# Rotary swap of queries and keys: from TensorE products with a permutation matrix to DMAs between partitions

## The chip, the cores and the metric

One core of one Trainium2 chip runs the whole program. The metric is the time of one execution on the device in microseconds, the median of several runs. Short names of the engines as the profile has them: PE (TensorE), DVE (VectorE), ACT (ScalarE), POOL (GpSimd), SP (SyncE, here only a queue of DMAs).

## What is computed

Two blocks one after the other on a sequence of 512 tokens of width 2048, in float32. The first, an mLSTM and a spatial gating unit with their projections, is not touched. The second has two hybrid layers over 528 tokens (16 meta tokens ahead): a long convolution, sliding window attention and a recurrent unit, side by side. The part around the change, cut to what matters:

```
def _partial_rotary(x, pos):                      # heads of 64, ROT_DIM = 16, half = 8
    ang = pos[:, None] * inv_freq[None, :]
    x1 = x[..., :half]
    x2 = x[..., half:ROT_DIM]
    rot = concatenate([x1 * cos - x2 * sin, x2 * cos + x1 * sin])
    return concatenate([rot, x[..., ROT_DIM:]])

q = _partial_rotary(q.reshape(B, L, N_HEADS, HEAD_DIM), pos)     # 16 heads
k = _partial_rotary(k.reshape(B, L, N_KV, HEAD_DIM), pos)        # 4 heads
att = _sliding_window_sink_attention(q, k, v, attn_sinks)
```

Only the first 16 features of each head are rotated: feature d is mixed with feature d + 8.

## The kernel before, in words

Features lie on partitions, tokens in the free dimension. A tile of 128 partitions holds two heads of 64, so the rotation mixes partitions 0 to 7 with 8 to 15 and 64 to 71 with 72 to 79.

Every projection is a run of *units*. A unit makes 256 output features in two passes of 128 (m = 0, 1), each over four *pieces* of the weights (j = 0 to 3, four tiles of 128 input features each). A product of two float32 numbers is made of three float32r products (`three`, L493 to L498), of a high and a low part of weights and inputs. SP loads the raw pieces (`load`), ACT rounds piece j to `w_high` (`high`, L884), DVE subtracts to get `w_low` (`low`, L1311), PE waits for that (`arrive`, L517) and multiplies. `high(U, j)` needs piece j of the unit before to be used up in both passes. With `wide=True` a pass has 96 products of 264 columns. ACT takes the sums out of PSUM (`take`, L898).

A layer first makes the keys (unit O_K) and values (O_V), then four groups of four heads each. Group g has the units V (queries), V+1 (convolution inputs), V+2 (attention gate), V+3 (recurrent inputs); V of the next group is the last unit, V+4, in the code of a group. The order of everything else is written out by hand on each engine. On PE small work is hung behind the pieces of these units by `hook` (`behind`, L806): at n = 8, behind piece 0 of unit V+1, `rotate(0)` and `rotate(1)`; at n = 11, behind piece 3 and so at the end of the first pass, the first `score` (L720); further scores, transposes (`turn`) and value products follow, one behind each piece; behind unit V+4 come the last of them and the products of the recurrent gates (`recur`).

The rotary step before: `rotate` (L707) multiplies both query tiles of a group, `qrw[:, t]`, by the permutation `rot`, whose entries are 1 and -1, into PSUM banks 4 to 7, four float32 products of 264 columns. DVE's `rope` (L1702) then multiplies that by `sin`, the tile by `cos`, and adds. `rotate_k` (L687) and the loop at L1636 do the same for the two tiles of keys, once in a layer.

On ACT a group begins at L1177: it takes query tile 0 out (L1178), copies values and keys for the products (`values`, `keys`), makes `w_high` of unit V+1 in between, takes query tile 1 out (L1185) and makes piece 3. Before that stand, from the group before, the two gates of the recurrent unit, tanh, exp and square root (L1232 to L1240). DVE's part of a group begins with the four `w_low` of unit V+1, then both ropes (L1712 to L1714). PE's loop over groups has three turns and one group behind it; ACT's has two turns of two groups. Both DMA queues are in use: SP's for weights, ACT's for the residual stream, constants and parameters of a layer.

`y2` (y_layer) holds the outputs of the layer, 16 tiles: Y_ATT 0 to 7, Y_LRU 8 to 11, Y_CONV 12 to 15.

Of the kernel before, what the change touches and what calls it, by code (L numbers as in the profile page):

```python
# [22 lines left out]
ALU = mybir.AluOpType  # L23
AX = mybir.AxisListType
ds = bass.ds

P = 128
# [17 lines left out]
LH = L // 2  # L45
# [4 lines left out]
HD = 64  # L50
NKV = 4
GROUP = 4
NH = NKV * GROUP
BLK = 128
# [23 lines left out]

K_IDENT, K_ONES, K_TRI, K_ROT = 0, P, 2 * P, 3 * P
K_MASK0 = 4 * P  # L80
K_MASK = K_MASK0 + NM + BLK
# [20 lines left out]
def program(nc, a, out):  # L102
# [14 lines left out]
    with ExitStack() as ctx:  # L117
# [102 lines left out]
        shape_at = rr.at  # L220
        kshape = rr.take("shape_constants", [P, K_ALL - K_ROT])
        rot = kshape[:, 0:P]
        ma0 = kshape[:, K_MASK0 - K_ROT:K_MASK - K_ROT]
        mas = kshape[:, K_MASK - K_ROT:K_CAUS - K_ROT]
        mca = kshape[:, K_CAUS - K_ROT:K_COS - K_ROT]
        cos = kshape[:, K_COS - K_ROT:K_SIN - K_ROT]
        sin = kshape[:, K_SIN - K_ROT:K_ALL - K_ROT]
        mo = rr.take("meta_out", [P, NM])
# [37 lines left out]
        def sem(name):  # L266
# [41 lines left out]
            sem("shape_in"), sem("pl_in"), sem("pl_tr"), sem("pl_ok"), sem("sink_in"))  # L308
        rot_mm, rope_done, rotk_mm, k_roped = sem("rot_mm"), sem("rope_done"), sem("rotk_mm"), sem("k_roped")
        kz_ready, vz_ready, mo_ready = sem("kz_ready"), sem("vz_ready"), sem("mo_ready")  # L310
# [181 lines left out]
        def _(pe):  # L492
# [185 lines left out]
            with pe.Fori(0, LAYERS) as l:  # L678
# [7 lines left out]

                def rotate_k():  # L687

                    pe.wait_ge(evac, 2 * (U + O_K) + 2)
                    pe.wait_ge(shape_in, 16 * (l + 1))  # L690
                    pe.wait_ge(pl_ok, l + 1)
                    for t in range(2):
                        for q in range(2):
                            last = pe.matmul(ps[:, 4 + 2 * t + q, 0:LH], rot, krw[:, t, q * LH:(q + 1) * LH], start=True, stop=True)
                        last.then_inc(rotk_mm, 1)

                unit_tokens(U + O_V, fill, 0, [
                    [(ps[:, i // 2, i % 2 * 256:(i % 2 + 1) * 256], NM + i * P) for i in range(ST)],
                    [(ps[:, 2, 0:256], 0)]], after=(rotate_k, None))
                unit(U + O_GRP, fill, wide=True)  # L700

                def group(g, ending=None):
# [3 lines left out]

                    def rotate(t):  # L707

                        if t == 0:
                            pe.wait_ge(evac, 2 * V + 2)  # L710
                            pe.wait_ge(k_roped, 2 * (l + 1))

                            pe.wait_ge(r_act, 2 * G)
                            pe.wait_ge(o_taken, 2 * G)
                            pe.wait_ge(mo_ready, 2 * G)
                        for q in range(2):
                            last = pe.matmul(ps[:, 4 + 2 * t + q, 0:LH], rot, qrw[:, t, q * LH:(q + 1) * LH], start=True, stop=True)
                        last.then_inc(rot_mm, 1)

                    def score(i, n):  # L720
                        q = qrw[:, i // 2, :]
                        bank = 4 + n % 2
                        if n == 0 and i == 0:
                            pe.wait_ge(rope_done, 2 * G + 2)
                            pe.wait_ge(kz_ready, G + 1)

                        pe.wait_ge(s_taken, 4 * A + 4 * i + n + 1)
                        tq = NM + n * BLK
                        w = NM + (2 if n else 1) * BLK
                        last = pe.matmul(ps[:, bank, 0:w], q[:, tq:tq + BLK], kz[:, i % 2, max(n - 1, 0), 0:w],  # L730
                                         start=True, stop=True)
                        if n == 0:
                            last = pe.matmul(ps[:, bank, 160:160 + NM], q[:, 0:BLK], kz[:, i % 2, 0, 0:NM],
                                             start=True, stop=True)
                        last.then_inc(s_done, 1)

                    def turn(i, n):
                        if n == 0:
                            pe.wait_ge(p_ready, A + i + 1)

# [65 lines left out]
                    def behind(first):  # L806

                        def hook(n):
                            n += first
                            if n == 8:  # L810
                                rotate(0)
                                rotate(1)
                            elif n >= 11:
                                step(n - 11)
                        return hook
# [67 lines left out]
        def _(act):  # L883
# [187 lines left out]
            with act.Fori(0, LAYERS) as l:  # L1071
# [6 lines left out]

                act.dma_start(kshape[:], consts[:, K_ROT:K_ALL]).then_inc(shape_in, 16)
                row = 0  # L1080
# [30 lines left out]
                act.wait_ge(res_out, 16 * (l + 1))  # L1111
                act.wait_ge(k_roped, 2 * (l + 1))

                def group(gp, s):
# [62 lines left out]
                    act.wait_ge(s_done, 4 * A)  # L1177
                    take(V, 0, two(qrw[:, 0, :]), halves(0))  # L1178
                    values()
                    high(V + 1, 0)  # L1180
                    keys(0)
                    high(V + 1, 1)
                    keys(1).then_inc(kz_ready, 1)
                    high(V + 1, 2)
                    take(V, 1, two(qrw[:, 1, :]), halves(2))  # L1185
                    high(V + 1, 3)
                    act.wait_ge(c_taken, G)
# [121 lines left out]
        def _(dve):  # L1309
# [299 lines left out]
            with dve.Fori(0, LAYERS) as l:  # L1609
# [26 lines left out]
                for m in range(2):  # L1636
                    k = krw[:, m, :]
                    dve.drain()
                    dve.wait_ge(rotk_mm, 2 * l + m + 1)
                    dve.tensor_tensor(two(t1[:]), halves(4 + 2 * m), two(sin), ALU.mult)  # L1640
                    dve.tensor_tensor(k, k, cos, ALU.mult)
                    dve.drain()
                    dve.tensor_tensor(k, k, t1[:], ALU.add).then_inc(k_roped, 1)  # L1643

                with dve.Fori(0, NKV) as g:
# [56 lines left out]
                    def rope(t):  # L1702

                        q = qrw[:, t, :]
                        dve.drain()
                        dve.wait_ge(rot_mm, 2 * G + t + 1)
                        dve.tensor_tensor(two(t1[:]), halves(4 + 2 * t), two(sin), ALU.mult)
                        dve.tensor_tensor(q, q, cos, ALU.mult)
                        dve.drain()
                        dve.tensor_tensor(q, q, t1[:], ALU.add).then_inc(rope_done, 1)  # L1710
# [140 lines left out]
def shape_constants():  # L1851
# [7 lines left out]
    half = HD // 4 // 2  # L1859
    for o in (0, HD):  # L1860
        for d in range(half):
            c[o + half + d, K_ROT + o + d] = -1.0
            c[o + d, K_ROT + o + half + d] = 1.0
    neg = np.float32(-1e30)
# [9 lines left out]
    for o in (0, HD):  # L1874
        for q in (0, half):
            c[o + q:o + q + half, K_COS:K_SIN] = np.cos(ang).T
            c[o + q:o + q + half, K_SIN:K_ALL] = np.sin(ang).T
    return c
# [22 lines left out]
```

## Time and profile before

| | |
|---|---|
| median of 3 runs | 3525.28 us (3524.44 to 3526.98) |
| the profiled execution, its own time | 3524.65 us |
| its span, first to last instruction | 3522.6 us |
| mean granted TensorE clock | 0.978 |
| busy: PE, DVE, ACT, POOL | 95%, 48%, 37%, 9% |
| the three products of `three`, each | 5280 instructions |
| DMA queue of ACT | 2592 packets, 19.18 MB, 1.4% |
| DMA queue of SP | 338944 packets, 281.09 MB, 26.2% |

How to read it: PE records overlap, since one product is fed in while the one before drains, so busy times of lines on PE add up to more than the span; the distance from start to start tells the cost. The two layers stand in the span at about 1800 to 2650 us and 2650 to 3480 us, their groups of heads at about 1900 to 2400 and 2740 to 3240 us.

### The profile page before, as it was taken

What the parts mean: (1) busy time and instruction counts of PE and PEld (TensorE: products, weight loads), DVE (VectorE), ACT (ScalarE), POOL (GpSimd) and SP (SyncE); (2) the same over time, 40 slices, a digit from 0 to 9 for tenths busy, and PEclk for the clock granted to TensorE, in tenths of its full rate; (3) what the DMA queues carried; (4) which work ended last, traced back from release to release, by engine and by line L of the source; (5) the groups of instructions that cost most, each with busy time, mean ns of one, the idle gap of its engine ahead of it and who ended that gap; (6) DMA issues with size and microseconds to landing.
All of it is one profiled execution on the core that took longest, in us unless ns stands there. A gap on an engine that the chain in (4) does not pass through costs nothing.

```text
span 3522.6 us, 58033 instructions
## 1 busy us (share of the span) xinstructions
PE 3354.9 (95%) x21518; PEld 3031.3 (86%) x21518; DVE 1702.0 (48%) x2289; ACT 1310.0 (37%) x2069; POOL 315.4 (9%) x320
## 2 busy tenths in 40 slices
PE   6999999999999999899969999999996999999996
PEld 5888988888888888788849999999996999999995
DVE  5332233334443434325683555556545455555555
ACT  3332233233333333323242554545224445545422
POOL 2000000000000000000000331330000214312000
PEclk9999999999999999999979999999997999999997
DMA  5332233233232323322213222223323222221421
GB/s 183 96 90 89 83 95 95 84 95 99 80 101 77 101 77 92 124 95 95 95 54 127 73 74 74 68 72 113 99 72 108 85 74 62 73 73 61 145 95 48
DMA packets 346082, 316.88 MB, mean 90 GB/s; under 512 B 18785, under 2 KB 339321, under 8 KB 344001
## 3 DMA queue, kind: packets, MB, share of 16 engines
q1 hardware_dynamic: 338944, 281.09, 26.2%
q10 hardware_dynamic: 2592, 19.18, 1.4%
q0 software_dynamic: 4400, 14.62, 1.2%
q8 instruction: 98, 1.61, 0.2%
q14 instruction: 48, 0.39, 0.0%
HBM read 297.74 MB, written 17.07 MB: 89 GB/s over the span
## 4 chain that ended last, share of the span: by engine, by line
PE 39%; issue 13%; DVE 3%; ACT 1%; DMA 1%; POOLq 1%; POOL 1%; DVEq 0%; ACTq 0%
PE ps L496 11%; PE ps L497 11%; PE ps L498 11%; PE ps L771 1%; PE ps L730 1%; DMA residual_stream<-y_layer 1%; DVE residual L1576 1%; DVE residual L1587 0%; PE ps L745 0%; PE ps L778 0%; PE ps L802 0%; PE ps L668 0%; PE ps L749 0%; DVE w_low L1314 0%; ACT x_high L1017 0%
## 5 line engine op out<-in xcount | busy, mean ns | idle before, releaser
L496 PE MATMUL ps<-x_high,w_high 128*128 128x264 f32 (+1 forms) x5280 | 1738.3, 329 | 65.9 <-DVE x_low L1595 47.5
L497 PE MATMUL ps<-x_low,w_high 128*128 128x264 f32 (+1 forms) x5280 | 1707.8, 323 | 0.0
L498 PE MATMUL ps<-x_high,w_low 128*128 128x264 f32 (+1 forms) x5280 | 1703.6, 323 | 0.0
L1314 DVE TENSOR_TENSOR w_low<-w_raw,w_high 128x1024 fp32r<-128x1024 f32 x524 | 640.7, 1230 | 1152.1 <-ACT w_high L890 1126.6
L496 PEld LDWEIGHTS ps<-x_high,w_high 128*128 128x128 f32 x5280 | 1000.5, 189 | 155.7 <-DVE x_low L1595 45.9
L497 PEld LDWEIGHTS ps<-x_low,w_high 128*128 128x128 f32 x5280 | 1000.7, 190 | 84.1 <-issue 3.8
L498 PEld LDWEIGHTS ps<-x_high,w_low 128*128 128x128 f32 x5280 | 997.3, 189 | 77.7
L890 ACT ACTIVATE w_high<-w_raw 128x1024 fp32r<-128x1024 f32 x524 | 551.7, 1058 | 730.6 <-PE ps L498 612.4
L502 PE MATMUL ps<-w_high,x_high 128*128 128x256 f32 x1184 | 333.1, 281 | 2.0 <-ACT w_spatial_rowsum L937 2.0
L503 PE MATMUL ps<-w_high,x_low 128*128 128x256 f32 x1184 | 333.1, 281 | 0.0
L504 PE MATMUL ps<-w_low,x_high 128*128 128x256 f32 x1184 | 333.0, 281 | 0.0
L502 PEld LDWEIGHTS ps<-w_high,x_high 128*128 128x128 f32 x1184 | 222.7, 188 | 3.7 <-issue 2.8
L504 PEld LDWEIGHTS ps<-w_low,x_high 128*128 128x128 f32 x1184 | 223.3, 189 | 0.0
L503 PEld LDWEIGHTS ps<-w_high,x_low 128*128 128x128 f32 x1184 | 222.6, 188 | 0.8
L1689 DVE SCALAR_TENSOR_TENSOR c_partial<-c_raw,par,c_partial 128x528 f32<-128x528 f32 x168 | 141.0, 839 | 30.3 <-issue 30.3
L901 ACT ACT_TABLE_LOAD x86 | 110.3, 1283 | 23.7 <-DVE k_roped L1643 11.8
L1657 DVE SCALAR_TENSOR_TENSOR p_block<-ps,shape_constants 128x272 f32<-128x272 f32 (+1 forms) x128 | 51.9, 406 | 136.5 <-PE ps L730 90.6
L427 POOL DMA_DIRECT2D gate_bc<-gate_rows x8 | 4.3, 532 | 1205.6 <-DVE y_m L1469 666.8
L473 POOL TENSOR_TENSOR y_layer<-y_layer,tmp 128x528 f32 x64 | 104.4, 1631 | 9.9 <-issue 9.9
L901 ACT ACTIVATE out_tmp_layer<-ps 128x528 f32<-128x528 f32 x32 | 19.3, 602 | 176.8 <-PE ps L498 176.8
L480 POOL TENSOR_TENSOR c_raw<-c_raw,a_gate_silu 128x528 f32<-128x528 f32 x8 | 8.9, 1118 | 791.1 <-ACT a_gate_silu L901 791.1
L471 POOL TENSOR_TENSOR tmp<-c_raw,par 128x528 f32<-128x528 f32 x64 | 78.1, 1220 | 14.5 <-issue 14.5
(331 smaller groups left out, 2623.9 us busy)
## 6 DMA issues: line engine op xcount, KB each, us to landing
w_raw<-in_w_in SPq DMA_DIRECT2D x776, 256.0 KB, 3.0
w_raw<-in_w_out SPq DMA_DIRECT2D x256, 256.0 KB, 2.9
residual_stream<-y_layer ACTq DMA_DIRECT2D x2, 4224.0 KB, 13.2
residual<-residual_stream ACTq DMA_DIRECT2D x8, 1056.0 KB, 11.5
x_natural<-in_x SPq DMA_DIRECT2D x4, 1024.0 KB, 8.8
x_feature_major<-x_stage POOLq DMA_DIRECT2D x16, 256.0 KB, 4.0
gate_bc<-gate_rows POOLq DMA_DIRECT2D x8, 512.0 KB, 4.5
acc<-x_feature_major POOLq DMA_DIRECT2D x1, 4096.0 KB, 13.3
```

What stands on the lines that cost most here:

```text
L471: pool.tensor_tensor(t1[:], cra[:, j:j + L], wj, ALU.mult)
L473: ins = pool.tensor_tensor(ct, ct, t1[:], ALU.add)
L496: pe.matmul(dst, wh[:, j, kt, wc], xh[:, k, tok], start=first, stop=False)
L497: pe.matmul(dst, wh[:, j, kt, wc], xl[:, k, tok], start=False, stop=False)
L498: return pe.matmul(dst, wl[:, j, kt, wc], xh[:, k, tok], start=False, stop=last)
L502: pe.matmul(dst, xh[:, k, tok], wh[:, j, kt, :], start=first, stop=False)
L503: pe.matmul(dst, xl[:, k, tok], wh[:, j, kt, :], start=False, stop=False)
L504: return pe.matmul(dst, xh[:, k, tok], wl[:, j, kt, :], start=False, stop=last)
L890: act.activation(wh[:, j], raw[:, j], ACT.Copy).then_inc(hi_ready, 1)
L901: act.activation(dst, src, fn, **kw).then_inc(evac, 1)
L1314: dve.tensor_tensor(wl[:, j], raw[:, j], f(wh[:, j]), ALU.subtract).then_inc(lo_ready, 1)
L1689: dve.scalar_tensor_tensor(cacc[:], cra[:, j:j + L], wj, cacc[:], ALU.mult, ALU.add)
```

## The change

The swap of partitions is made by DMAs from SBUF to SBUF, issued by ACT. For a tile, `swap` issues four: 8 rows of 528 floats each, from rows 8 to 15 to rows 0 to 7 and back, for both heads of the tile. They go into rows of `y2` that are free at that time: Y_ATT + 2g + t for query tile t of group g (semaphore `q_swapped[t]`, 64 for a tile), Y_LRU + m for key tile m (`k_swapped`, 128 for both). ACT drains after each `take` of queries and then issues the four. The signs of the permutation move into the constants (`-sin` in the upper rows of each head), rows of the tile that aren't swapped meet a sine of zero. DVE reads the swapped tile from `y2` rather than from PSUM. PE loses `rotate` and `rotate_k`; the waits in them go or move to `score` and `turn`. ACT's wait for `k_roped` moves from ahead of the groups to ahead of `keys(0)`. The constants loaded in a layer are 128 columns fewer.

```diff
@@ tensor
-                def rotate_k():
-                    pe.wait_ge(evac, 2 * (U + O_K) + 2)
-                    pe.wait_ge(shape_in, 16 * (l + 1))
-                    pe.wait_ge(pl_ok, l + 1)
-                    for t in range(2):
-                        for q in range(2):
-                            last = pe.matmul(ps[:, 4 + 2 * t + q, 0:LH], rot, krw[:, t, q * LH:(q + 1) * LH], start=True, stop=True)
-                        last.then_inc(rotk_mm, 1)
...
-                    def rotate(t):
-                        if t == 0:
-                            pe.wait_ge(evac, 2 * V + 2)
-                            pe.wait_ge(k_roped, 2 * (l + 1))
-                            pe.wait_ge(r_act, 2 * G)
-                            pe.wait_ge(o_taken, 2 * G)
-                            pe.wait_ge(mo_ready, 2 * G)
-                        for q in range(2):
-                            last = pe.matmul(ps[:, 4 + 2 * t + q, 0:LH], rot, qrw[:, t, q * LH:(q + 1) * LH], start=True, stop=True)
-                        last.then_inc(rot_mm, 1)
...
                             pe.wait_ge(rope_done, 2 * G + 2)
                             pe.wait_ge(kz_ready, G + 1)
+                            pe.wait_ge(pl_ok, l + 1)
+                            pe.wait_ge(r_act, 2 * G)
...
                         if n == 0:
+                            pe.wait_ge(mo_ready, 2 * G)
                             pe.wait_ge(p_ready, A + i + 1)
...
-                            if n == 8:
-                                rotate(0)
-                                rotate(1)
-                            elif n >= 11:
+                            if n >= 11:
                                 step(n - 11)
@@ scalar
-                act.wait_ge(k_roped, 2 * (l + 1))
+                def swap(dst, src, done):
+                    for o in (0, HD):
+                        for a0, a1 in ((0, RD), (RD, 0)):
+                            act.dma_start(dst[o + a0:o + a0 + RD, :], src[o + a1:o + a1 + RD, :]).then_inc(done, 16)
+                for m in range(2):
+                    swap(y2[:, Y_LRU + m, :], krw[:, m, :], k_swapped)
...
                     take(V, 0, two(qrw[:, 0, :]), halves(0))
+                    act.drain()
+                    swap(y2[:, ds(Y_ATT + 2 * g, 1), :].squeeze(1), qrw[:, 0, :], q_swapped[0])
                     values()
                     high(V + 1, 0)
+                    act.wait_ge(k_roped, 2 * (l + 1))
                     keys(0)
                     high(V + 1, 1)
                     keys(1).then_inc(kz_ready, 1)
                     high(V + 1, 2)
                     take(V, 1, two(qrw[:, 1, :]), halves(2))
+                    act.drain()
+                    swap(y2[:, ds(Y_ATT + 2 * g + 1, 1), :].squeeze(1), qrw[:, 1, :], q_swapped[1])
                     high(V + 1, 3)
@@ vector, the same for the keys with k_swapped, 128 * (l + 1)
                         q = qrw[:, t, :]
                         dve.drain()
-                        dve.wait_ge(rot_mm, 2 * G + t + 1)
-                        dve.tensor_tensor(two(t1[:]), halves(4 + 2 * t), two(sin), ALU.mult)
+                        dve.wait_ge(q_swapped[t], 64 * (G + 1))
+                        dve.tensor_tensor(t1[:], y2[:, ds(Y_ATT + 2 * g + t, 1), :].squeeze(1), sin, ALU.mult)
@@ constants
-            c[o + q:o + q + half, K_SIN:K_ALL] = np.sin(ang).T
+            c[o + q:o + q + half, K_SIN:K_ALL] = np.sin(ang).T if q else -np.sin(ang).T
```

## Rows read from the trace of the kernel before

**Rows 1.** Page, part 1: busy us (share of the span) and instructions by engine
```profile
PE 3354.9 (95%) x21518; PEld 3031.3 (86%) x21518; DVE 1702.0 (48%) x2289; ACT 1310.0 (37%) x2069; POOL 315.4 (9%) x320
```

**Rows 2.** Timeline (start us, duration us, instruction), PE around the keys' rotation
```profile
1888.37 0.28 PE L504 MATMUL ps<-w_low,x_high 128*128 128x256 f32 x1
...
1890.38 0.28 PE L503 MATMUL ps<-w_high,x_low 128*128 128x256 f32 x1
```

**Rows 3.** Timeline of ACT, group 1 to 2 of layer one
```profile
2165.13 0.59 ACT L901 ACTIVATE q_roped<-ps 128x528 f32<-128x528 f32 x1
2165.62 1.05 ACT L890 ACTIVATE w_high<-w_raw 128x1024 fp32r<-128x1024 f32 x1
```

**Rows 4.** Timeline of DVE there: w_low pieces 0 and 3, ropes' first and last
```profile
2160.61 1.23 DVE L1314 TENSOR_TENSOR w_low<-w_raw,w_high 128x1024 fp32r<-128x1024 f32 x1 [3.20 <-ACT w_high L890]
...
2166.70 1.23 DVE L1314 TENSOR_TENSOR w_low<-w_raw,w_high 128x1024 fp32r<-128x1024 f32 x1 [0.22 <-ACT w_high L890]
2168.19 0.71 DVE L1707 TENSOR_TENSOR tmp<-ps,shape_constants 128x528 f32<-128x528 f32 x1 [0.26 <-PE ps L717]
...
2171.86 0.71 DVE L1710 TENSOR_TENSOR q_roped<-q_roped,tmp 128x528 f32<-128x528 f32 x1
```

**Rows 5.** Timeline of PE there: first product of V+1, first score
```profile
2161.90 0.39 PE L496 MATMUL ps<-x_high,w_high 128*128 128x264 f32 x1 [2.95 <-DVE w_low L1314]
...
2176.66 0.41 PE L730 MATMUL ps<-k_zero_padded,q_roped 128*128 128x144 f32 x2
```

**Rows 6.** Waits of PE, 1880 to 3200 us: total us, times, longest
```profile
PE ps L717 <- ACT q_roped L901: 2.4, 3, 1.0
```

**Rows 7.** Timeline of ACT's queue: DMA issues at the start of layer one
```profile
1856.19 1.09 ACTq L1087 DMA_DIRECT2D par_rows_layer<-in_lru_conv_b  x1
...
1860.38 0.26 ACTq L1087 DMA_DIRECT2D par_rows_layer<-in_lru_lambda  x1
1860.81 0.36 ACTq L1089 DMA_DIRECT2D small<-in_attn_sinks  x1
```

**Rows 8.** Timeline of ACT: an activation behind a drain
```profile
2027.69 0.74 ACT L1236 ACTIVATE r_tanh<-r_gate_a,small 128x528 f32<-128x528 f32 x1 [0.17 <-issue]
```

**Rows 9.** Windows (stretch, length, busy by engine, PEclk, DMA), group 1 to 2, layer two
```profile
2997.60:3015.40 17.80, 15.18 (x107) 14.73 (x106) 8.96 (x10) 7.49 (x20) 0.00 (x0) 0.90 0.40 120
```

**Rows 10.** Timeline of DVE, layer one: last rope and w_low piece 0, other groups
```profile
1926.81 0.71 DVE L1710 TENSOR_TENSOR q_roped<-q_roped,tmp 128x528 f32<-128x528 f32 x1
...
2036.57 1.23 DVE L1314 TENSOR_TENSOR w_low<-w_raw,w_high 128x1024 fp32r<-128x1024 f32 x1
...
2047.61 0.71 DVE L1710 TENSOR_TENSOR q_roped<-q_roped,tmp 128x528 f32<-128x528 f32 x1
...
2280.66 1.22 DVE L1314 TENSOR_TENSOR w_low<-w_raw,w_high 128x1024 fp32r<-128x1024 f32 x1
...
2291.63 0.71 DVE L1710 TENSOR_TENSOR q_roped<-q_roped,tmp 128x528 f32<-128x528 f32 x1
```

**Rows 11.** Timeline of PE, layer one: starts of V+1 and first scores, other groups
```profile
1932.53 0.41 PE L730 MATMUL ps<-k_zero_padded,q_roped 128*128 128x144 f32 x2
...
2039.85 0.36 PE L496 MATMUL ps<-x_high,w_high 128*128 128x264 f32 x1 [1.68 <-DVE w_low L1314]
...
2053.33 0.41 PE L730 MATMUL ps<-k_zero_padded,q_roped 128*128 128x144 f32 x2
...
2296.40 0.41 PE L730 MATMUL ps<-k_zero_padded,q_roped 128*128 128x144 f32 x2
```

**Rows 12.** Timeline of ACT, layer one: last copy of values, first copy of keys
```profile
1897.17 0.36 ACT L901 ACTIVATE v_tokens<-ps 128x256 f32<-128x256 f32 x1
...
1911.62 1.01 ACT L1125 ACTIVATE k_zero_padded<-k_roped 64x256 f32 x3
```

**Rows 13.** DMA issues by line: count, KB each, median us from issue to landing
```profile
residual<-residual_stream ACTq DMA_DIRECT2D x8, 1056.0 KB, 11.5
...
w_x_diag<-in_lru_wx POOLq DMA_DIRECT2D x16, 16.0 KB, 1.9
```

More of the change, by code:

```diff
@@ L52 @@
 GROUP = 4
+RD = HD // 8
 NH = NKV * GROUP
@@ L76 @@
 Y_ATT, Y_LRU, Y_CONV = 0, 8, 12
-K_IDENT, K_ONES, K_TRI, K_ROT = 0, P, 2 * P, 3 * P
-K_MASK0 = 4 * P
+K_IDENT, K_ONES, K_TRI = 0, P, 2 * P
+K_MASK0 = 3 * P
 K_MASK = K_MASK0 + NM + BLK
@@ L220, in program @@
         shape_at = rr.at
[L221 to L227, printed above, removed]
+        kshape = rr.take("shape_constants", [P, K_ALL - K_MASK0])
+        ma0 = kshape[:, K_MASK0 - K_MASK0:K_MASK - K_MASK0]
+        mas = kshape[:, K_MASK - K_MASK0:K_CAUS - K_MASK0]
+        mca = kshape[:, K_CAUS - K_MASK0:K_COS - K_MASK0]
+        cos = kshape[:, K_COS - K_MASK0:K_SIN - K_MASK0]
+        sin = kshape[:, K_SIN - K_MASK0:K_ALL - K_MASK0]
         mo = rr.take("meta_out", [P, NM])
@@ L308, in program @@
             sem("shape_in"), sem("pl_in"), sem("pl_tr"), sem("pl_ok"), sem("sink_in"))
-        rot_mm, rope_done, rotk_mm, k_roped = sem("rot_mm"), sem("rope_done"), sem("rotk_mm"), sem("k_roped")
+        q_swapped, rope_done, k_swapped, k_roped = [sem(f"q_swapped{t}") for t in range(2)], sem("rope_done"), sem("k_swapped"), sem("k_roped")
         kz_ready, vz_ready, mo_ready = sem("kz_ready"), sem("vz_ready"), sem("mo_ready")
@@ L685, in _ @@
                 pe.transpose(ps[:, 5, 0:ROWS_L2], prow2[0:ROWS_L2, 1, :], ident[0:ROWS_L2, 0:ROWS_L2]).then_inc(pl_tr, 1)
-                def rotate_k():
-                    pe.wait_ge(evac, 2 * (U + O_K) + 2)
-                    pe.wait_ge(shape_in, 16 * (l + 1))
-                    pe.wait_ge(pl_ok, l + 1)
-                    for t in range(2):
-                        for q in range(2):
-                            last = pe.matmul(ps[:, 4 + 2 * t + q, 0:LH], rot, krw[:, t, q * LH:(q + 1) * LH], start=True, stop=True)
-                        last.then_inc(rotk_mm, 1)
                 unit_tokens(U + O_V, fill, 0, [
                     [(ps[:, i // 2, i % 2 * 256:(i % 2 + 1) * 256], NM + i * P) for i in range(ST)],
-                    [(ps[:, 2, 0:256], 0)]], after=(rotate_k, None))
+                    [(ps[:, 2, 0:256], 0)]])
                 unit(U + O_GRP, fill, wide=True)
@@ L1077, in _ @@
                 act.dma_start(x_res, y2[:]).then_inc(res_out, 16)
-                act.dma_start(kshape[:], consts[:, K_ROT:K_ALL]).then_inc(shape_in, 16)
+                act.dma_start(kshape[:], consts[:, K_MASK0:K_ALL]).then_inc(shape_in, 16)
                 row = 0
@@ L1638, in _ @@
                     dve.drain()
-                    dve.wait_ge(rotk_mm, 2 * l + m + 1)
-                    dve.tensor_tensor(two(t1[:]), halves(4 + 2 * m), two(sin), ALU.mult)
+                    dve.wait_ge(k_swapped, 128 * (l + 1))
+                    dve.tensor_tensor(t1[:], y2[:, Y_LRU + m, :], sin, ALU.mult)
                     dve.tensor_tensor(k, k, cos, ALU.mult)
@@ L1859, in shape_constants @@
     half = HD // 4 // 2
[L1860 to L1863, printed above, removed]
+    assert half == RD
     neg = np.float32(-1e30)
```

## The prediction

> **What bounds the kernel now.** I read the page first: PE is busy for 95% of the span [rows 1], so a change counts only where PE works less or stands longer. The edit touches one stage, the attention groups of the two layers (from about 1850 to 2300 us and again from 2690 to 3140 us), so the rest was read there: PE's timeline around the products that go, PE's waits, then ACT's, DVE's and PE's timelines of the same places side by side. The reader is to see two things. First, the price of a rotation on PE: the last ordinary product before the rotation of the keys starts at 1888.37 and the pitch is 0.12; the second ordinary one after it starts at 1890.38, where it would have started at 1888.61 [rows 2]. So 1.77 us for four fp32 products and the change over to them and back. The rotation of a group's queries shows the same. Second, who is late where the groups change. In the first group of a layer ACT waits for PE between its pieces. In the other three ACT has just finished the gates of the group before, and takes the queries out, copies keys and makes w_high one behind the other without a pause: the second q_roped at 2165.13, w_high piece 3 at 2165.62, before the copy has ended [rows 3]. DVE's first w_low starts at 2160.61 and ends 1.23 later, at 2161.84 [rows 4], and PE, idle for 2.95 us, starts at 2161.90 [rows 5]: PE hangs on ACT there. PE then also waited for q_roped before three of the eight rotations, 2.4 us in all [rows 6].
>
> **What goes.** On PE one rotation of keys and four of queries in each layer: ten times 1.77, at most 17.7 us, and the 2.4 us of waits. The waits that stood in `rotate` move to `score` and `turn`; each but `rope_done` is for something finished long before. DVE's three products per half stay as they are; the operand read from PSUM is read from SBUF, and 0.71 us for the form with the PSUM operand (L1707) stands beside 0.71 for the one with both in SBUF (L1710) [rows 4], so I take no difference.
>
> **What comes.** All of it on ACT's queue. After each of the two q_roped copies of a group: a drain, then four DMA issues, then the work that was next. ACT's own queue shows what an issue costs: a transfer of 4 rows took 0.26 us, one of 128 rows 0.36, with 0.1 to 0.2 of register work between them; behind large transfers in flight the form of 4 rows took 1.09 [rows 7]. Nothing large is in flight on that queue in the groups, and a swap has 8 rows, so I take 0.27 and 0.1 for registers: 0.37 from one issue to the next. A drain shows as 0.17 of idle time between two activations [rows 8]. So d, by which the next operation of ACT comes later: the copy must end (0.59), drain 0.17, four issues 1.48, restart 0.1, together 2.34; before, the next one started 0.49 after the copy's start [rows 3]. d = 1.9 us. Its bounds: issues every 0.28, d = 1.4; every 1.09, d = 4.7. The drain matters, because without it issues could run under a copy.
>
> **Where d is on the path.** Two clocks run from a group change to its first score (L730): PE's, from its first product of unit V+1 through 96 products, and the ropes', ACT's copies, w_low piece 3, then two ropes on DVE. The score starts at the later one. The first d shifts everything that ACT does; the second shifts w_high piece 3 and so w_low piece 3, and the ropes stand behind that on DVE. So the ropes end 2d = 3.8 later, less some 0.1 that DVE no longer waits for PE's rotation (its wait of 0.26 before 2168.19 against 0.17 for a drain) [rows 4].
>
> Group 1 to 2 (called change 2): w_low piece 0 ends at 2161.84 + 1.9 = 2163.7; PE's way from there to the score was 14.76, of it 1.77 rotation and 1.0 the wait before it, leaving 12.0 [rows 5, 6]: 2175.7. Ropes: 2171.86 + 0.71 + 3.7 = 2176.3 [rows 4]. PE's idle time before V+1 grows from 3 to 5 us, and in layer two the same place, with a shorter pause, was followed by products at half pace: mean granted clock 0.90 over that 17.8 us [rows 9], that is 3.4 us at 1.2 instead of 2.4 GHz and 1.5 to 1.7 us lost. I count that loss in both layers now: PE 2177.2, against 2176.66 before, +0.5. In layer two it was already there; the first d and the rotation cancel: 0. Together +0.5.
>
> Change 1 (group 0 to 1): ropes 2047.61 + 0.71 + 3.7 = 2052.0, PE 2053.33 - 1.77 = 2051.6 [rows 10, 11]. PE's start of V+1 does not move, because it started at 2039.85, while w_low piece 0 had ended at 2036.57 + 1.23 = 2037.8, 2.0 us ahead: PE's loop jumps back there. Saved 2053.33 - 2052.05 = 1.3, twice: -2.5. Change 3: ropes 2291.63 + 0.71 + 3.7 = 2296.05, PE 2280.66 + 1.23 + 1.9 + 12.0 = 2295.8, against 2296.40 [rows 10, 11]: -0.3, twice: -0.6.
>
> First group: ACT has pauses, so only the second d counts: ropes end by 1926.81 + 0.71 + 1.9 = 1929.4, while PE comes at 1932.53 - 1.77 = 1930.8 [rows 10, 11]. All 1.77 is gained, twice: -3.5. If that cover of 1.4 us is gone, each us more costs one.
>
> Keys: eight issues after v_tokens (ends 1897.5), so until 1900.6; landed by 1903; both ropes 4.4 (as the queries' from 2168.19 to 2172.57 [rows 4]): 1907.4. First needed by the key copies at 1911.62 [rows 12]. Cover 4 us; -1.77 twice: -3.5.
>
> The landing of a swap: 16 KB by the nearest small transfers took 1.9 us, 1056 KB took 11.5 [rows 13]; a swap is four of 16.5 KB, so 2 to 3 us from the last issue. The second swap's last issue is at about 2165.72 + 1.9 + 1.65 = 2169.3, and the second rope wants it at 2168.19 + 2.27 + 3.7 = 2174.2: 4.9 us of cover, which is why I count the transfer itself at nothing.
> By the Trainium skill ("DMA: Bandwidth & Descriptors", section "Anatomy of one DMA", measured for GpSimd's path) a DMA has a fixed cost of about 2.0 us, most of it the write receipt, and its bandwidth section wants transfers batched, those under 64 KB being dominated by descriptors; that speaks against moving 16 rows in four pieces, and the trace's 1.9 us agrees with the fixed part. Overlapped, it would change nothing here; one behind the other it is the third rival below.
>
> **Sum** against the profiled run's own 3524.65 us (span 3522.6): -3.5 (keys) -3.5 (first group) -2.5 +0.5 -0.6 = -9.6, so 3515.0. The median of the runs is 0.6 above the profiled one: 3515.6. Of the 20.1 us that PE gets back, half is handed to ACT.
>
> **Rivals.**
> 1. Forecast, issues at 0.33 to 0.45 us: 3510 to 3521, taken 3515.6. Chance 0.46.
> 2. Dearer issues, slower than before: ACT's queue at the three late changes. With d = 4.7 the ropes end 9.3 later: change 1 +4.3, change 2 +5.2, change 3 +5.2, first group -0.3, keys -1.8: +12.6 a layer, 3550. The three late changes give 12 us for each us of d; the sum is zero at d = 2.8, an issue of 0.61, and 7 us slower at 0.75. For it: nine of twelve such transfers cost about 1 us (one is shown) [rows 7]; against: those stood behind 5 MB. Chance 0.13.
> 3. The four transfers don't overlap: 4 x 1.9 = 7.6 us after the drain, the second rope starts 1.2 later than DVE could, six times: +7; keys 8 x 1.9 hold ACT's key copies by 6 us and the first score by 1.5: +3. Together 3525, no change. Against: issues come every 0.37 us and other queues have many in flight. Chance 0.09. This is what the batching rule would make of it.
> 4. Clock: after 5 us of idle time PE stays at half speed twice as long at change 2, or drops at change 3 too (idle 1.7 there): 1.5 to 1.7 us for each of two to four places beyond the cover of the ropes (0.7): 3518.5 to 3521, no change. Chance 0.13.
> 5. Cheaper, d = 1.4: change 1 gives the full 1.77, change 3 1.3, change 2 0.8: 3508. Chance 0.19.
>
> **Numbers.** A measurement of this kernel tells about 0.2% (7 us) from no change; faster means below 3518.2. Faster: nine tenths of 1 and all of 5 less a little, 0.58. Same: the rest of 1, 3 and 4, 0.28. Slower: 2 and some of 3, 0.14. Range 3507 to 3530: from the cheap case to an issue of about 0.7 us; only the worse part of 2 and what is better than 5 is left out.
>
> **What would show it.** Right: no L694 or L717; PE's idle time before V+1 about 5 us at change 2 and about 1.7 at change 3; DMA issues of about 0.3 us on ACT's queue with a hole of some 2.3 us after each q_roped; a short wait of PE L730 for DVE's ropes in three of four groups; DVE never long waiting for a swap. Wrong: ropes that wait for DMA (3), issues of over 0.6 (2), no wait before L730 and PE's idle time as before (5), more than 7 us of granted clock 0.5 in the groups of a layer (4). The sum falls as a whole if ACT can issue under its copies, or if its pause at the jump back of its own loop (change 2) grows with the longer code.

## The result, and the profile after

The changed kernel takes 3537.1 us (median of 7 runs, 3536.5 to 3539.7); the kernel before took 3525.3 in the runs between them (7 runs, 3524.3 to 3529.3). The ratio is 1.0033, 95% interval 1.0021 to 1.0044: 0.33% slower, where 0.27% faster was forecast, and outside of the range of 3507 to 3530. The profiled run has a span of 3535.5 us against 3522.6.

The page of the kernel after, its span and part 1 (answers [rows 1]):

```profile
span 3535.5 us, 57971 instructions
PE 3348.4 (95%) x21438; PEld 3024.7 (86%) x21438; DVE 1703.0 (48%) x2289; ACT 1310.7 (37%) x2069; POOL 315.4 (9%) x320
```

The rotations are gone, ten with four float32 products each; the trace shows a float32 product as two records, so eighty are missing, and PE is busy for 6.5 us less. Nothing else on that page names the loss: ACT is not busier, because a DMA issue is not counted as busy. One has to look at the places where the groups change. The same change from group 1 to 2 as in [rows 3], timeline of ACT in the kernel after (start us, us, instruction, idle time before and its releaser):

```profile
2159.08 0.61 ACT L878 ACTIVATE q_roped<-ps 128x528 f32<-128x528 f32 x1
2159.85 3.05 ACTq L1094 DMA_DIRECT2D y_layer<-q_roped  x4
2163.04 0.42 ACT L1119 ACTIVATE v_zero_padded<-v_tokens 128x256 f32 x1 [3.35 <-issue]
...
2169.49 0.59 ACT L878 ACTIVATE q_roped<-ps 128x528 f32<-128x528 f32 x1
2170.24 3.03 ACTq L1094 DMA_DIRECT2D y_layer<-q_roped  x4
2173.38 1.06 ACT L867 ACTIVATE w_high<-w_raw 128x1024 fp32r<-128x1024 f32 x1 [3.30 <-issue]
```

Four issues hold ACT's queue for 3.05 us; 77 of the 80 in the trace last 0.67 to 0.72 us (the others 0.76, 0.80 and 1.16), and with the register instruction between them they start every 0.775 us. The forecast had 0.37. The operation behind the first copy starts 3.96 us after it, where it started 0.49 after it before [rows 3]: d is 3.47 here for the first half and 3.89 - 0.49 = 3.40 for the second, against 1.9 in the forecast. In what follows d is taken as 3.44, the mean of the two.

DVE there (answers [rows 4]), from w_low piece 0 to the end of the ropes:

```profile
2164.98 1.23 DVE L1304 TENSOR_TENSOR w_low<-w_raw,w_high 128x1024 fp32r<-128x1024 f32 x1 [6.55 <-ACT w_high L867]
...
2174.47 1.23 DVE L1304 TENSOR_TENSOR w_low<-w_raw,w_high 128x1024 fp32r<-128x1024 f32 x1 [3.63 <-ACT w_high L867]
2176.09 0.71 DVE L1697 TENSOR_TENSOR tmp<-y_layer,shape_constants 128x528 f32<-128x528 f32 x1 [0.39 <-issue]
...
2179.82 0.71 DVE L1700 TENSOR_TENSOR q_roped<-q_roped,tmp 128x528 f32<-128x528 f32 x1
```

And PE there (answers [rows 5]), and PE's waits of the whole run:

```profile
2166.26 0.59 PE L496 MATMUL ps<-x_high,w_high 128*128 128x264 f32 x1 [6.30 <-DVE w_low L1304]
...
2180.93 0.51 PE L709 MATMUL ps<-k_zero_padded,q_roped 128*128 128x144 f32 x2 [1.41 <-DVE q_roped L1700]
```

```profile
PE ps L496 <- DVE w_low L1304: 22.9, 6, 6.3
...
PE ps L709 <- DVE q_roped L1700: 9.6, 6, 2.0
```

The reader is to see the hole of ACT twice. The first opens PE's wait for w_low (6.3 us here; all such waits of the run were 8.8 us and are 22.9 now), the second makes w_low piece 3 late, and the ropes behind it, so that PE waits at the first score too, in all six late groups. DVE itself does not wait for a swap: the 0.39 us before the first rope is "issue", no DMA. At the keys the wait is for DMA, and it is covered (timelines of ACT and DVE, kernel after):

```profile
1897.55 5.69 ACTq L1094 DMA_DIRECT2D y_layer<-k_roped  x8
```

```profile
1904.73 0.71 DVE L1630 TENSOR_TENSOR tmp<-y_layer,shape_constants 128x528 f32<-128x528 f32 x1 [6.40 <-DMA y_layer<-k_roped]
```

Where the 12.9 us of span came from, by the time of each group's first score in the two traces (after less before, and the step from one score to the next):

| place | layer one | layer two | forecast, each |
|---|---|---|---|
| keys and first group | -3.4 | -3.5 | -3.5 |
| change 1 | +2.7 | +2.9 | -1.25 |
| change 2 | +3.35 | +3.4 | +0.5, 0 |
| change 3 | +3.7 | +3.7 | -0.3 |

That is +12.8. Beside it stand +1.6 before 1850 us, in work that both kernels share, +1.6 in layer one's last group, where the granted clock is 0.5 for 3.4 us, and -1.4 between the layers and -1.8 behind the second one; they sum to nothing.

### The profile page after: what moved, and what is told of

The parts are those of the page before. It is cut to its first block, busy times and chain, and to the rows that moved or that the text cites. A ratio compares the mean times of both kernels' runs of the same rounds, so it can differ in the third digit from the quotient of the medians.

```text
span 3535.5 us, 57971 instructions
## 1 busy us (share of the span) xinstructions
PE 3348.4 (95%) x21438; PEld 3024.7 (86%) x21438; DVE 1703.0 (48%) x2289; ACT 1310.7 (37%) x2069; POOL 315.4 (9%) x320
## 4 chain that ended last, share of the span: by engine, by line
PE 39%; issue 14%; DVE 3%; ACT 1%; DMA 1%; POOLq 1%; POOL 1%; DVEq 0%; ACTq 0%
PE ps L496 11%; PE ps L497 11%; PE ps L498 11%; PE ps L751 1%; PE ps L709 1%; DMA residual_stream<-y_layer 1%; DVE residual L1566 1%; DVE residual L1577 0%; PE ps L725 0%; PE ps L758 0%; PE ps L782 0%; PE ps L668 0%; PE ps L729 0%; DVE w_low L1304 0%; ACT x_high L994 0%
## 5 line engine op out<-in xcount | busy, mean ns | idle before, releaser
L709 PE MATMUL ps<-k_zero_padded,q_roped 128*128 128x272 f32 (+1 forms) x256 | 73.4, 368 | 9.6 <-DVE q_roped L1700 9.6
## 6 DMA issues: line engine op xcount, KB each, us to landing
residual_stream<-y_layer ACTq DMA_DIRECT2D x2, 4224.0 KB, 13.2
residual<-residual_stream ACTq DMA_DIRECT2D x8, 1056.0 KB, 11.7
```

## The experiments

Theory: ACT's queue is held by the issues, at a price of 0.775 us for each, and all of the loss is in the two holes of each group. Rivals: the transfers or their landing; the drains; what was taken away from PE (its clock, the waits that were moved). Medians of before in the sessions below are 3526.3 to 3527.3; ratios are against the runs of the same session.

**Take the swaps away.** In the changed kernel:

```diff
-                    act.drain()
-                    swap(y2[:, ds(Y_ATT + 2 * g, 1), :].squeeze(1), qrw[:, 0, :], q_swapped[0])
...
-                        dve.wait_ge(q_swapped[t], 64 * (G + 1))
+                        dve.wait_ge(evac, 2 * V + t + 1)
```

> The changed kernel without its DMA swaps and without the two drains before them; DVE waits only for the copy q_roped (or k_roped) itself and reads whatever stands in y_layer, so the swap is left out of the computation. It shows what taking the rotation off PE is worth by itself. Theory (the whole loss is the time that ACT spends issuing): ten rotations of 1.77 us and up to 2.4 us of waits come back, nothing else moves: 18 to 20 us faster than the kernel before, 3505 to 3507 us. Rival (PE gets nothing from the missing products, because the ropes or the clock take it): within 8 us of before, 3517 or more.

Measured: 3506.2 us, ratio 0.9941 (0.9924 to 0.9957). As the theory has it: the rotation on PE was worth 21 us, and the additions take more than that back.

**Add the swaps alone**, to the kernel before:

```diff
+                    act.drain()
+                    swap(y2[:, ds(Y_ATT + 2 * g, 1), :].squeeze(1), qrw[:, 0, :], q_swapped[0])
...
                         dve.wait_ge(rot_mm, 2 * G + t + 1)
+                        dve.wait_ge(q_swapped[t], 64 * (G + 1))
```

> The kernel before, its PE rotation kept and still used, with the drains and all DMA swaps added on ACT's queue; DVE waits for both. It shows the cost of the additions alone. Theory: the next operation of ACT comes 3.4 us later twice in each group; the late changes give, in each layer, about +1.8 (change 1), +5.0 (change 2, of it 1.6 for clock), +3 (change 3), and 0 to +1.5 in the first group, the keys hidden: 20 to 23 us slower, 3545 to 3548 us. Rival (the loss comes from what was taken away, for instance waits moved to the score, or from PE's emptier queue and its clock): within 5 us of before.

Measured: 3545.9 us, ratio 1.0055 (1.0038 to 1.0072). With PE's rotation in place the additions cost 19 us, and PE's waits for w_low are the 22.9 us of the changed kernel, though nothing was taken from PE. What was removed or moved on PE is no cause: taking it away is a gain with the swaps (3545.9 to 3537.1) as without them. But the two effects don't add up; -21 and +19 would make -2, where the change measures +12. With the rotation PE comes to the first score late enough never to wait there; without it 17.7 us of products go and the 9.6 us of waits at the score come.

**Half of the issues:**

```diff
-                    for o in (0, HD):
+                    for o in (0,):
```

> The changed kernel with two of the four DMAs of each swap (the second head's rows are not swapped, which leaves half of the swap out). Theory (each issue holds ACT 0.775 us, so d falls from 3.44 to 1.9 us, and each us of d is worth 12 us): 3516 us, 3512 to 3520. Rival (a fixed part of the swap, its drain, the wait for the landing or the restart of ACT, carries the loss): less than half of the difference between the changed kernel and no_swaps goes, 3522 to 3535 us.

Measured: 3518.6 us, ratio 0.9977 (0.9967 to 0.9986), inside the theory's range. Timeline of ACT in this kernel, from group 0 to 1:

```profile
2030.63 0.59 ACT L878 ACTIVATE q_roped<-ps 128x528 f32<-128x528 f32 x1
2031.38 1.49 ACTq L1094 DMA_DIRECT2D y_layer<-q_roped  x2
2033.02 0.42 ACT L1119 ACTIVATE v_zero_padded<-v_tokens 128x256 f32 x1 [1.79 <-issue]
```

d is 2.39 - 0.49 = 1.9 here, the value that the forecast took for four issues, and the gain over the kernel before is 8.1 us by the ratio, where the forecast had 9.7. The hole is 0.30 us longer than its issues, with two of them (1.79 and 1.49) as with four (3.35 and 3.05): that is all that is left for the drain and the restart, so the drain is not the loss; no run takes it out alone. Three points give the slope, each taken against the kernel before of its own session: -20.8 us at d = 0, -8.1 at 1.9, +11.6 at 3.44. The first 1.9 us cost 6.7 us each and the next 1.54 cost 12.8 each. So the "12 us for each us of d" was right where all three late changes hang on it, and the point of no change lies at 1.9 + 8.1/12.8 = 2.5, where the forecast had 2.8.

**The same transfers from another queue.** SP issues them, behind its loads of unit V+1; ACT neither drains nor issues. The keys' swaps go to SP as well, behind the loads of the values, and go out at 1866 rather than at 1897.55, so they too are hidden:

```diff
+                    for m in range(2):
+                        sp.wait_ge(evac, 2 * V + m + 1)
+                        swap(y2[:, ds(Y_ATT + 2 * g + m, 1), :].squeeze(1), qrw[:, m, :], q_swapped[m])
```

> The changed kernel with the same sixteen-row swaps issued from SP's queue instead of ACT's; ACT neither drains nor issues, SP waits for each copy. Theory (ACT's issue time, not the transfers): ACT's copies, w_high and w_low run as in the kernel before, the swap of the second half lands some 4.5 us after its copy ends, about when DVE's second rope could start, so nearly all of the gain stays: 3505 to 3511 us. Rival (the transfers themselves, their landing or the traffic of 8-row pieces cost the time): 3525 to 3537 us, as in the changed kernel. A second rival: SP's weight loads, now behind the swaps in its queue, come late, and PE waits for them: 3515 us or more, with PE's new waits on weights.

Measured: 3503.3 us, ratio 0.9934 (0.9917 to 0.9950), some 2 us under the theory's range, below the kernel before by 24 us in the medians and, by the two ratios, below the changed one by 35, with the whole computation in it. It is even a little under the kernel without swaps, whose clock fell at change 2 in both layers, where here it did not; at change 1 it fell here in both layers, there in one. PE's waits for w_low, timelines of SP and of DVE at change 2, kernel with swaps on SP:

```profile
PE ps L509 <- DVE w_low L1304: 9.5, 4, 2.7
```

```profile
2154.79 9.91 SPq L355 DMA_DIRECT2D y_layer<-q_roped  x8
2165.05 1.21 SPq L349 DMA_DIRECT2D w_raw<-in_w_in  x2
```

```profile
2162.54 1.23 DVE L1304 TENSOR_TENSOR w_low<-w_raw,w_high 128x1024 fp32r<-128x1024 f32 x1 [0.22 <-ACT w_high L880]
2164.15 0.71 DVE L1697 TENSOR_TENSOR tmp<-y_layer,shape_constants 128x528 f32<-128x528 f32 x1 [0.39 <-issue]
...
2166.48 0.71 DVE L1697 TENSOR_TENSOR tmp<-y_layer,shape_constants 128x528 f32<-128x528 f32 x1 [0.22 <-issue]
```

The issues are no cheaper on SP (0.65 to 0.74 us each); they hold a queue that has time. The second swap's last issue ends at about 2164.7, and the second rope starts at 2166.48 without a wait. The price is that the loads of unit V+2 now go out at 2165.05, over 7 us after w_low piece 0 ended (2157.69), where they were issued 0.2 us after it before; PE doesn't wait for weights anywhere in these groups. So the transfers, their landing and their traffic cost nothing, and the rival of transfers one behind the other falls with them.

**Which hole does what.** The swap of one half on ACT as in the change, that of the other half and the keys' on SP:

```diff
                     take(V, 0, two(qrw[:, 0, :]), halves(0))
+                    act.drain()
+                    swap(y2[:, ds(Y_ATT + 2 * g, 1), :].squeeze(1), qrw[:, 0, :], q_swapped[0])
```

> The changed kernel with the first half's swap (and its drain) on ACT's queue as in the change, and the keys' and the second half's from SP's queue. Theory (two clocks): one d of 3.44 us ahead of w_high piece 0 shifts both PE's start of the next unit and the ropes. Against the kernel with all swaps on SP: change 1 +0.2, change 2 +3.4 to 5, change 3 +2.7 in each layer: 3516 to 3520 us. If only the sum of the issues counted, wherever they stand, both halves would give the same, about 3514.

> The changed kernel with the second half's swap (and its drain) on ACT's queue, and the keys' and the first half's from SP's queue. Theory (two clocks): this d stands behind PE's start, and only w_high piece 3, w_low piece 3 and the ropes come 3.44 us later. Against all swaps on SP: change 1 +0.2, change 2 +2.0, change 3 +1.1 in each layer: 3508 to 3512 us. If only the sum of the issues counted: about 3514, as with the first half.

Measured: first half on ACT 3525.0 us, ratio 0.9993 (0.9984 to 1.0003); second half 3517.1, ratio 0.9971 (0.9961 to 0.9982). Both miss their numbers by 5 us or more; equal they are not. PE at change 2 of layer one, first with the first half's swap on ACT:

```profile
2162.10 0.59 PE L509 MATMUL ps<-x_high,w_high 128*128 128x264 f32 x1 [6.45 <-DVE w_low L1312]
...
2176.05 0.41 PE L722 MATMUL ps<-k_zero_padded,q_roped 128*128 128x144 f32 x2
```

then with the second half's on ACT:

```profile
2159.55 0.39 PE L509 MATMUL ps<-x_high,w_high 128*128 128x264 f32 x1 [2.70 <-DVE w_low L1312]
...
2174.41 0.51 PE L722 MATMUL ps<-k_zero_padded,q_roped 128*128 128x144 f32 x2 [2.08 <-DVE q_roped L1708]
```

These are the two clocks of the prediction, one at a time. The first hole stands ahead of PE's start (6.45 us of waiting, none at the score), the second behind it (2.70 as before, and 2.08 at the score). The ratios put the first half at 21 us over the kernel with all swaps on SP and the second at 13, together 34 of the 35 that both cost. The sizes that were expected were off for these reasons. After the long pause the first kernel needs 13.95 us from 2162.10 to the score, where the kernel with all swaps on SP needs 11.71. Windows of the two (stretch, length, busy by engine, PEclk, DMA):

```profile
2162.10:2176.00 13.90, 13.90 (x96) 13.90 (x97) 7.75 (x9) 4.72 (x10) 0.00 (x0) 0.82 0.38 112
```

```profile
2154.00:2169.40 15.40, 12.74 (x105) 12.53 (x105) 8.97 (x10) 8.41 (x22) 0.00 (x0) 1.00 0.23 64
```

So the clock took 2.2 us there and, by the same two times, 2.5 in layer two, against the 0 to 1.6 that I had allowed; and 1.5 us of the first kernel's time lie behind the last score of layer two, where its granted clock is 0.5 for 3.4 us and that of the kernel with swaps on SP is not. In the second kernel the ropes cost more than worked out. They had less room than I took: in the kernel with swaps on SP they end 0.87 us ahead of the score at change 2 and 1.19 at change 3, where +2.0 and +1.1 from a d of 3.44 need 1.4 and 2.3. From their end to a score that waits for them are 0.35 to 0.5 us, which I had at nothing, and change 3 of layer one has a stretch of half clock (1.6 us) ahead of it.

**Issues under a running activation.** The four issues moved behind the next w_high, the drain replaced by a wait for the copy:

```diff
-                    act.drain()
-                    swap(y2[:, ds(Y_ATT + 2 * g, 1), :].squeeze(1), qrw[:, 0, :], q_swapped[0])
                     values()
                     high(V + 1, 0)
+                    act.wait_ge(evac, 2 * V + 1)
+                    swap(y2[:, ds(Y_ATT + 2 * g, 1), :].squeeze(1), qrw[:, 0, :], q_swapped[0])
```

> The changed kernel with each query swap's four issues moved behind the next w_high piece (piece 0 for the first half, piece 3 for the second), and in place of the drain a wait for the copy's own semaphore. If ACT's sequencer issues DMAs while an activation runs, some 1 us of the 3.1 of issues lies under w_high and the drain's tail is gone: d falls from 3.44 to about 2.1 for each half and piece 3 of w_high is no longer behind the second swap at all, so the ropes come some 4 us earlier: 3512 to 3520 us. If an issue cannot overlap a running activation, d stays over 3 and only the second half's moves behind piece 3: 3522 to 3530 us.

Measured: 3511.8 us, ratio 0.9956 (0.9939 to 0.9973), at the lower end of the first range. ACT at change 2:

```profile
2156.24 0.61 ACT L878 ACTIVATE q_roped<-ps 128x528 f32<-128x528 f32 x1
2156.75 0.41 ACT L1119 ACTIVATE v_zero_padded<-v_tokens 128x256 f32 x1
2156.98 0.72 ACTq L1094 DMA_DIRECT2D y_layer<-q_roped  x1
...
2157.58 1.06 ACT L867 ACTIVATE w_high<-w_raw 128x1024 fp32r<-128x1024 f32 x1
2157.82 2.23 ACTq L1094 DMA_DIRECT2D y_layer<-q_roped  x3
2160.27 1.03 ACT L1110 ACTIVATE k_zero_padded<-k_roped 64x256 f32 x3 [1.63 <-issue]
```

The first issue starts while the small copies run and the next under w_high: the queue goes on past an activation that has been handed over. The hole shrinks to 1.63 us, and w_high piece 0 is no longer behind it. Without leaving ACT, 27 of the changed kernel's 32 us over the kernel without swaps are back (by the ratios), and the issues are as many and each as dear. Place and drain were changed together here; what each gives was not measured. What is still missing against the swaps on SP is in part the landing, which is no longer hidden: DVE waits for the second half's swap before its second rope in all eight groups (10.2 us in all, up to 1.9 us; 0.95 at change 2), and PE waits 4.1 us at the score.

**What makes an issue dear.** Thirteen more DMAs of other forms behind the keys' eight swaps, one line each:

```diff
+                act.dma_start(y2[0:8, Y_LRU + 2, :], krw[8:16, 0, :]).then_inc(k_swapped, 16)
+                act.dma_start(y2[16:20, Y_LRU + 2, :], krw[8:12, 0, :]).then_inc(k_swapped, 16)
...
+                act.dma_start(y2[:, Y_CONV + 3, :], x_res[:, 0, :]).then_inc(k_swapped, 16)
```

> The changed kernel with thirteen more DMAs on ACT's queue behind the eight of the keys, each of another form and all into parts of y_layer or DRAM that nobody reads; DVE waits for them too. They are, in order, between buffers on the chip: 8 rows of 528 numbers, 4 rows, 1 row, 16 rows, 128 rows of 528, 8 rows of 512, 8 rows of 128, 4 rows of 128, 128 rows of 128; then 4 rows of 128 and 8 rows of 528 from DRAM, 8 rows of 528 to DRAM, 128 rows of 528 from DRAM. It prices one issue by its form. Theory 1 (the price is in what is described, rows and their length): few rows are cheap, 16 rows of 528 dearer than 8, 128 rows dearest. Theory 2 (the price is in the source, on the chip or in DRAM): all from the chip cost 0.65 to 0.7 us and those from DRAM 0.27 to 0.37. Theory 3 (few rows are cut into pieces for the 16 DMA engines, and that costs): the forms with fewer than 16 rows cost 0.65, those of 16 and 128 rows 0.27 to 0.37. The time of the whole is about 10 us a layer above the changed kernel at most, and is not what is asked.

> The kernel with the thirteen further forms again, now in the opposite order and ahead of the keys' eight swaps: first 128 rows of 528 from DRAM, 8 rows of 528 to DRAM, 8 rows of 528 from DRAM, 4 rows of 128 from DRAM, and then the nine between buffers on the chip. Theory 1 (the price is in the form: DRAM at one end cheap, both ends on the chip dear): the first four 0.27 to 0.5 us, the nine and the eight swaps 0.56 to 0.73 us, as in the other order. Theory 2 (what came cheap was cheap because it stood last, or behind a DMA of another kind): the first four cost 0.5 to 0.8 us now, and those that stand last come down towards 0.3.

Timeline of ACT's queue, first order; the lines L1099 to L1111 are the thirteen forms in the order of the expectation (`residual_stream` and `spare` lie in DRAM):

```profile
1895.94 5.69 ACTq L1095 DMA_DIRECT2D y_layer<-k_roped  x8
1901.66 0.67 ACTq L1099 DMA_DIRECT2D y_layer<-k_roped  x1
...
1903.03 0.61 ACTq L1101 DMA_DIRECT2D y_layer<-k_roped  x1
1903.67 0.61 ACTq L1102 DMA_DIRECT2D y_layer<-k_roped  x1
1904.30 0.61 ACTq L1103 DMA_DIRECT2D y_layer<-k_roped  x1
...
1906.42 0.64 ACTq L1106 DMA_DIRECT2D y_layer<-k_roped  x1
1907.09 0.56 ACTq L1107 DMA_DIRECT2D y_layer<-k_roped  x1
1907.68 0.50 ACTq L1108 DMA_DIRECT2D y_layer<-residual_stream  x1
1908.22 0.30 ACTq L1109 DMA_DIRECT2D y_layer<-residual_stream  x1
1908.56 0.32 ACTq L1110 DMA_DIRECT2D spare<-k_roped  x1
1908.90 0.37 ACTq L1111 DMA_DIRECT2D y_layer<-residual_stream  x1
```

The opposite order, where L1097 is the last form of the other order and L1109 its first:

```profile
1895.53 0.39 ACTq L1097 DMA_DIRECT2D y_layer<-residual_stream  x1
1895.95 0.36 ACTq L1098 DMA_DIRECT2D spare<-k_roped  x1
1896.34 0.32 ACTq L1099 DMA_DIRECT2D y_layer<-residual_stream  x1
1896.69 0.31 ACTq L1100 DMA_DIRECT2D y_layer<-residual_stream  x1
1897.03 0.62 ACTq L1101 DMA_DIRECT2D y_layer<-k_roped  x1
...
1902.44 0.70 ACTq L1109 DMA_DIRECT2D y_layer<-k_roped  x1
```

In both orders a DMA with DRAM at one end takes 0.30 to 0.39 us to issue, be it 8 rows or 128, in or out; the one of 4 rows took 0.31, and 0.50 right behind a copy on the chip. A DMA from one buffer on the chip to another takes 0.56 to 0.73, for 1, 4, 8, 16 and 128 rows alike. Layer two repeats this within 0.04 us in both runs, but for one row: the last form of the first order, 128 rows from DRAM, took 1.26 us there and 0.37 in layer one, for which nothing in the runs gives the reason. So neither the rows (theory 1 of the first run), nor a cut into pieces (its theory 3), nor the place in the queue (theory 2 of the second) sets the price; where both ends lie does. That on-chip sources as such are dear, as theory 2 of the first run put it, is wrong by one row: 8 rows from the chip to DRAM cost 0.32. The times of the whole, 3545.4 and 3544.0 in one run each, say nothing more.

## Why the prediction was wrong

**The step that failed is the price of one issue.** I took 0.27 from the 4-row loads of [rows 7] and 0.1 for registers. Those loads come from DRAM; the change's transfers have both ends on the chip, and no such DMA stood in the trace of before. I had asked how many rows a form has and what is in flight, and not where it comes from. Four times 0.775 instead of 0.37 makes d 3.5 instead of 1.9; measured are 3.40 to 3.47 at change 2. The bounds, 0.28 and 1.09, held it; the value taken between them was that of the row nearest in size.

**The sum follows from it.** By the prediction's own price, -9.6 + 12 x (3.44 - 1.9) = +8.9 us; the four kinds of place together measured +12.8, 3.9 more. At change 2 of layer one: the ropes ended at 2172.57 before; the 0.9 us by which the group began late and two d of 3.47 and 3.40 put them at 2180.4, and they end at 2180.53. The score is 0.40 later. That 0.40, six times 2.4 us of the 3.9, was left out: a term of the sum, the time from DVE's last rope to PE's score, had not been priced because PE had never waited there. Another 1.0 us is in the second hole at changes 1 and 3, where 0.3 us more pass before the fourth issue (3.33 us for the four rather than 3.03) and d is 3.69, four times 0.25; the reason isn't shown, and 0.5 us stay open. Rival 2 is what happened, with its mechanism, its place and its deciding point (an issue of 0.61; d = 2.5 by the runs makes it 0.53). Its chance of 0.13 was too low, and its own time of 3550 too high, for it was priced at 1.09. (Two slips stand in that working: the sum's own zero is at 1.9 + 9.6/12 = 2.7 rather than 2.8, and issues every 0.28 make d 1.5, not 1.4.)

**What held.** The gain on PE: forecast 17.7 and up to 2.4 us of waits, 21 measured without swaps. Keys and first group: -7.0 forecast, -6.9 measured, but this came out with luck, for both terms stood on the cheap issue too. The keys' last issue ends at 1903.24 where 1900.6 was forecast; their ropes end at 1909.05, and the first key copy, late by a d of its own, starts at 1913.34 without a wait. The first group's cover of 1.4 us is used up: its ropes end at 1930.23, PE's product ahead of the score starts at 1930.44 and the score at 1930.72. The two clocks, and that each d counts twice in the ropes. DVE's products cost the same from the buffer as from PSUM (0.71). The landing is hidden, and rival 3 is out. The Trainium skill ("DMA: Bandwidth & Descriptors", "Anatomy of one DMA") puts about 2.0 us on a DMA; from the keys' last issue to DVE's start are 2.2 us here, counted from the issue's start, and 1.5 from its end, which agrees roughly, and as forecast that is not what the change costs.

**The clock (rival 4)** came too, and cost less than feared: the granted clock is 0.5 for 17 us in layer one's groups and 13.7 in layer two's, where the kernel before had none and 3.4. From PE's start to the score, less the wait at the score, the changed kernel takes 13.1 to 13.3 us at the three changes of layer one, against 11.7 at full clock. But this lies under PE's wait for the ropes and is not paid twice; only the 1.6 us in the last group is. Where the ropes are early, as with the first half's swap alone on ACT, it is paid in full.

## What to carry to other kernels

Price a DMA that you add by a row whose two ends lie where its ends lie, not by one of its size; if the trace has none, the bounds are the forecast, and the change should be put where the dear end does no harm. Then ask which queue issues it: the same 80 transfers cost 32 us on the engine that hands weights to PE and nothing on SP, whose loads could go out 7 us later without a wait of PE. If they must stay on the engine, put them behind an operation that is already handed over, with a wait for the data's own semaphore instead of a drain, and look whether they still land in time.

## What was not expected of the hardware

An issue of a DMA between two on-chip buffers takes 0.56 to 0.73 us of ACT's queue, with 1 row or 128; with DRAM at one end, 0.30 to 0.39. On SP only the swap's form was run, at 0.65 to 0.74 with one of 0.84. Single issues of over 1 us stand beside these: 1.16 for a swap in the changed kernel, 1.26 for 128 rows from DRAM, and 1.09 behind large transfers [rows 7]. The reasons aren't shown. A pause of PE of about 3 us, from the start of one product to that of the next, was followed by half clock in some runs and not in others: 2.94 us without a drop at change 2 (swaps on SP), 3.18 with one (no swaps), and in the kernel before 3.2 us without one in layer one and 2.9 with one in layer two. Shorter pauses, at change 1 of layer one, are no different: 2.04 us with a drop (second half's swap on ACT) and 2.38 with one (swaps on SP), 2.02 without (no swaps) and 1.96 without (before); PE needs 13.2 us to the score after the two drops and 11.7 in the kernel without swaps. No length of the pause tells the two apart here, so a forecast can only carry the 1.5 to 2.5 us as a chance.
